# Moving softmax, mask, split and load work in a two-layer hybrid trunk kernel on one core

## The reference: a trunk of two layers

```
for l in range(DEPTH):                       # DEPTH = 2
    x = x + 0.5 * swiglu(rms_norm(x), ...)   # ffn 0, ffn 2
    h = rms_norm(x)
    x = x + (mixer_mla_gdn(h, ...) if l % 2 == 0 else mixer_spatial_gating(h, ...))
    x = x + 0.5 * swiglu(rms_norm(x), ...)   # ffn 1, ffn 3
```

## Time and profile before

| | |
|---|---|
| runs before | median 1094.08 us (1093.31, 1094.08, 1097.67) |
| profiled execution | 1093.22 us, span 1091.2 us, so 2.0 us around it |
| busy in the span | PE 1065.9 us (98%), DVE 637.0 (58%), ACT 514.2 (47%), POOL 49.8 (5%) |
| granted TensorE clock | 0.998 on the mean |
| first mixer | about 201 to 374 us of the span |
| spatial gating | about 752 us on |

### The profile page before, as it was taken

How to read it: one execution, slowest core, us unless ns; L and a number is a source line. 1 busy time by engine, 2 the same in 40 slices (tenths; PEclk the granted TensorE clock), 3 DMA queues, 4 the chain that set the end, 5 groups by cost and what they waited for, 6 DMA issues and landing times.

```text
span 1091.2 us, 18956 instructions
## 1 busy us (share of the span) xinstructions
PE 1065.9 (98%) x8393; PEld 969.9 (89%) x8393; DVE 637.0 (58%) x783; ACT 514.2 (47%) x619; POOL 49.8 (5%) x32
## 2 busy tenths in 40 slices
PE   7999999999888999999999999999999999999998
PEld 7999988998777799998889999887788889999986
DVE  5756543699753675555457655435665547555542
ACT  6644433585673454443345444334665436444430
POOL 1000000110172000000000000001000000000000
PEclk9999999999999999999999999999999999999999
DMA  9856555253005276655538555554554465655531
GB/s 311 268 184 191 193 191 175 92 196 117 2 4 157 78 232 193 193 183 177 184 113 254 178 188 192 194 182 149 192 173 172 165 221 187 187 176 187 191 115 39
DMA packets 127194, 184.88 MB, mean 169 GB/s; under 512 B 4205, under 2 KB 101722, under 8 KB 126986
## 3 DMA queue, kind: packets, MB, share of 16 engines
q1 hardware_dynamic: 126368, 181.85, 51.3%
q0 software_dynamic: 448, 1.71, 0.5%
q10 hardware_dynamic: 298, 0.12, 0.1%
HBM read 182.62 MB, written 1.05 MB: 168 GB/s over the span
## 4 chain that ended last, share of the span: by engine, by line
PE 92%; DVE 4%; issue 2%; ACT 1%; DMA 0%; POOLq 0%; ACTq 0%; POOL 0%; DVEq 0%
PE banks L1337 21%; PE banks L1338 20%; PE banks L1339 20%; PE banks L1378 7%; PE banks L1382 7%; PE banks L1379 7%; PE banks L1735 1%; PE banks L1461 1%; PE banks L1462 1%; PE banks L1463 1%; PE banks L1425 1%; PE banks L1958 1%; DVE wlo L889 1%; DVE arena L1209 1%; DMA pos_rows<-in_positions 0%
## 5 line engine op out<-in xcount | busy, mean ns | idle before, releaser
L889 DVE TENSOR_TENSOR wlo<-raw,whi 128x2048 fp32r<-128x2048 f32 (+1 forms) x167 | 383.4, 2302 | 228.1 <-ACT whi L466 228.0
L466 ACT ACTIVATE whi<-raw 128x2048 fp32r<-128x2048 f32 (+1 forms) x171 | 324.1, 1908 | 382.0 <-PE banks L1339 241.8
L1337 PE MATMUL banks<-xTh,whi 128*128 128x256 f32 x1408 | 397.4, 282 | 1.0 <-DVE wlo L1011 0.9
L1338 PE MATMUL banks<-xTl,whi 128*128 128x256 f32 x1408 | 396.5, 282 | 0.0
L1339 PE MATMUL banks<-xTh,wlo 128*128 128x256 f32 x1408 | 396.5, 282 | 0.0
L1337 PEld LDWEIGHTS banks<-xTh,whi 128*128 128x128 f32 x1408 | 266.2, 189 | 1.7 <-issue 1.3
L1338 PEld LDWEIGHTS banks<-xTl,whi 128*128 128x128 f32 x1408 | 266.3, 189 | 0.0
L1339 PEld LDWEIGHTS banks<-xTh,wlo 128*128 128x128 f32 x1408 | 266.3, 189 | 0.0
L1378 PE MATMUL banks<-whi,hTh 128*128 128x512 f32 x336 | 133.4, 397 | 0.0
L1379 PE MATMUL banks<-wlo,hTh 128*128 128x512 f32 x336 | 132.3, 394 | 0.0
L1382 PE MATMUL banks<-whi,hTl 128*128 128x512 f32 x336 | 105.5, 395 | 0.0
(11 more groups left out here) (249 smaller groups left out, 988.9 us busy)
## 6 DMA issues: line engine op xcount, KB each, us to landing
raw<-in_ffn_w_up SPq DMA_DIRECT2D x44, 1024.0 KB, 5.6
raw<-in_ffn_w_down SPq DMA_DIRECT2D x44, 1024.0 KB, 4.9
raw<-in_ffn_w_gate SPq DMA_DIRECT2D x43, 1024.0 KB, 5.4
raw<-in_sg_w_in SPq DMA_DIRECT2D x16, 1024.0 KB, 5.5
raw<-in_ab_w_in SPq DMA_DIRECT2D x8, 1024.0 KB, 5.2
raw<-in_sg_w_out SPq DMA_DIRECT2D x8, 1024.0 KB, 5.2
raw<-in_ab_w_out SPq DMA_DIRECT2D x4, 1024.0 KB, 4.8
raw<-in_ab_w_in SPq DMA_DIRECT2D x2, 832.0 KB, 4.4
```

Source lines behind the costliest of these rows:

```text
L466: A(whi[:, j % SLOTS, 0:kt * width], raw[:, j % SLOTS, 0:kt * width], ACT.Copy).then_inc(S("hi_ready"), 1)
L889: TT(wlo[:, j % SLOTS, 0:n], raw[:, j % SLOTS, 0:n], whi[:, j % SLOTS, 0:n].bitcast(f32), ALU.subtract).then_inc(S("lo_ready"), 1)
L1337: mm(out_ap, lh, rh, start=first, stop=False)
L1338: mm(out_ap, lh, rl, start=False, stop=False)
```

## The change

1. ACT runs a one-column exponent right after its last SiLU of the convolutions, so that the exponent's table is loaded there, and the last copy `nt_out(5)` moves behind the first head's exponents.
2. DVE takes the sums of gates ahead of `head_sums(1)`, and takes each head's maxima one step earlier than before.
3. The masked blocks of L are made straight from PSUM banks 5 and 2; ACT's copies of L are gone. Two blocks stand at h = 4, the other eight after the last head. The seed of DT for the second tile uses banks 3 and 6, and PE's second `gram` moves behind the last head's values.
4. SP releases the loads of ffn 1 at `o_sums` 2, the middle of the scan.
5. POOL splits b+16 and b+17 in place of DVE. ACT makes the high part of b+16 ahead of the copies of the last transposes (`yT_hi(4, 8)`). PE's eight groups have the feature block outside, so that it is done with b+12 after four groups instead of six.
6. `ws_raw` moves to other memory and is loaded and masked after the first mixer (`x_updated` 8) instead of before the second one. Its memory overlaps `v_norm_row`, which is now loaded after `wsT_ready` 2.

```diff
-        ws_raw = at(0, GROUPS, P)
+        ws_raw = at(R0 + 2912, GROUPS, P)
...
-        DT_SEED_BANKS = ((3, 6), (5, 2))
-        POOL_LO = [u_ab + 12, u_ab + 13, u_ab + 14, u_ab + 15]
+        DT_SEED_BANKS = ((3, 6), (3, 6))
+        POOL_LO = [u_ab + i for i in range(12, 18)]
...
-                sp_.wait_ge(S("w_sums"), 1)
+                sp_.wait_ge(S("o_sums"), 2)
...
             pool_lo(u_ab + 15)
+            pool_lo(u_ab + 16)
+            pool_lo(u_ab + 17)
...
-            pool.wait_ge(S("x_updated"), 16)
-            load(v_norm_row, bc(sg_norm, [P, SGW]), "sg_loaded")
+            pool.wait_ge(S("x_updated"), 8)
             load(ws_raw, sg_ws[0].rearrange("g i j -> i g j"), "sg_loaded")
-            pool.wait_ge(S("sg_loaded"), 32)
+            pool.wait_ge(S("sg_loaded"), 16)
             nc.gpsimd.tensor_tensor(ws_raw, ws_raw, bc(const("tril128").unsqueeze(1), [P, GROUPS, P]),
                                     ALU.mult).then_inc(S("ws_masked"), 1)
+            pool.wait_ge(S("x_updated"), 16)
+            pool.wait_ge(S("wsT_ready"), 2)
+            load(v_norm_row, bc(sg_norm, [P, SGW]), "sg_loaded")
...
             conv_silu(5)
-            nt_out(5)
+            A(rope_tmp[:, 0, 0, 0:1], ones128[:, 0:1], ACT.Exp).then_inc(S("gate_exps"), 1)
...
             exps(0)
+            nt_out(5)
             exps(1)
...
-                if h == 5:
-                    act.wait_ge(S("score_sums"), HEADS)
-                    for t in range(NT):
-                        act.wait_ge(S("seed_sums"), t + 1)
-                        A(LT[:, 512 * t:512 * t + 512], B[(5, 2)[t]][:], ACT.Copy).then_inc(S("seed_ready"), 1)
...
+            hi(b + 16)
             yT_hi(4, 8)
-            for j in range(16, 18):
-                hi(b + j)
+            hi(b + 17)
...
             row_max(1)
-            head_sums(1)
...
-            row_max(2)
             gcf, ekf = (a.rearrange("p t h -> p (t h)") for a in (gc, ek))
...
+            head_sums(1)
+            row_max(2)
...
+            head_norm(QKVn[1], 1, 1.0).then_inc(S("k_normed"), 1)
+            row_max(3)
...
+            def masked_block(t, n):
+                dve.wait_ge(S("seed_sums"), t + 1)
+                if n == 4:
+                    dve.wait_ge(S("score_sums"), HEADS)
+                TT(LT_LEVEL[n][t].rearrange("p (m j) -> p m j", j=64),
+                   B[(5, 2)[t]][:].rearrange("p (m j) -> p m j", j=64), eight(f"level{LEVELS[n]}"), ALU.mult
+                   ).then_inc(S("lt_level"), 1)
...
-                if 0 < h < HEADS - 2:
+                if 1 < h < HEADS - 2:
                     row_max(h + 2)
...
+                    masked_block(0, 0)
+                    masked_block(0, 1)
+
+            for n in range(2, 5):
+                masked_block(0, n)
             for n in range(5):
-                for t in range(NT):
-                    TT(LT_LEVEL[n][t].rearrange("p (m j) -> p m j", j=64), h3(LT, t), eight(f"level{LEVELS[n]}"), ALU.mult
-                       ).then_inc(S("lt_level"), 1)
+                masked_block(1, n)
...
             yT_lo(4, 8)
-            for j in range(16, 18):
-                lo(b + j)
             next_x(2, [1.0, 1.0])
...
-                if h == 7:
-                    pe.wait_ge(S("seed_ready"), 4)
-                    gram(qT, (6, 7))
             weighted_values(HEADS - 1)
+            pe.wait_ge(S("seed_ready"), 4)
+            gram(qT, (6, 7))
...
-            pe.wait_ge(S("seed_ready"), 6)
+            pe.wait_ge(S("lt_level"), 5)
             m1(0, 0)
+            pe.wait_ge(S("lt_level"), 10)
             m1(0, 1)
...
-            for t in range(NT):
-                for kk in range(4):
+            for kk in range(4):
+                for t in range(NT):
```

More of the change, by code:

```diff
@@ L1145, in _ @@
             row_max(1)
-            head_sums(1)
-            dve.wait_ge(S("head_sums"), 2)
-            both = qk_head_ss.rearrange("p a m -> p (a m)")
-            link(rsqrt(both, both, 2 * M, 1.0))
-            def head_norm(a, i, scale):
-                a3 = a.rearrange("p t (h d) -> p (t h) d", d=DK)
-                return STT(a3, a3, scale, bc(qk_head_ss[:, i, :].unsqueeze(2), [P, M, DK]), ALU.mult, ALU.mult)
-            head_norm(QKVn[1], 1, 1.0).then_inc(S("k_normed"), 1)
-            row_max(2)
             gcf, ekf = (a.rearrange("p t h -> p (t h)") for a in (gc, ek))
@@ L1165, in _, with head_norm @@
             ins.then_inc(S("gc_ready"), 1)
+            head_sums(1)
+            row_max(2)
+            dve.wait_ge(S("head_sums"), 2)
+            both = qk_head_ss.rearrange("p a m -> p (a m)")
+            link(rsqrt(both, both, 2 * M, 1.0))
+            def head_norm(a, i, scale):
+                a3 = a.rearrange("p t (h d) -> p (t h) d", d=DK)
+                return STT(a3, a3, scale, bc(qk_head_ss[:, i, :].unsqueeze(2), [P, M, DK]), ALU.mult, ALU.mult)
+            head_norm(QKVn[1], 1, 1.0).then_inc(S("k_normed"), 1)
+            row_max(3)
             m3 = lambda a: a.rearrange("p (m j) -> p m j", j=64)
@@ L1204, in _ @@
                         TT(h3(D, t), eight("eye64"), h3(D, t), ALU.subtract).then_inc(S("d_ready"), 1)
-            dve.wait_ge(S("seed_ready"), 2)
+                    masked_block(0, 0)
+                    masked_block(0, 1)
+            for n in range(2, 5):
+                masked_block(0, n)
             for n in range(5):
-                for t in range(NT):
-                    TT(LT_LEVEL[n][t].rearrange("p (m j) -> p m j", j=64), h3(LT, t), eight(f"level{LEVELS[n]}"), ALU.mult
-                       ).then_inc(S("lt_level"), 1)
+                masked_block(1, n)
             dve.wait_ge(S("exp_done"), 2 * HEADS)
@@ L1745, in m1 @@
             def m1(n, t):
-                pe.wait_ge(S("lt_level"), 2 * n + t + 1)
+                pe.wait_ge(S("lt_level"), 5 * t + n + 1)
                 quadrants(t, (M1_BANKS if n else M1_FIRST)[t], LT_LEVEL[n], natural, by_t(D), d_at(n), flips(9), flips(n)
```

## The result

| | before | changed |
|---|---|---|
| first comparison | 1093.97 us median (1092.70 to 1100.66, 10 runs) | 1102.32 us (1099.14 to 1104.68, 10 runs) |
| ratio, 95% interval | | 1.0055 [1.0036, 1.0073], +6.0 us [3.9, 8.0] |
| profiled execution | 1093.22 us, clock 0.998 | 1102.91 us, span 1101.1 us, clock 0.994 |

Slower, clear of noise, and in all three comparisons by more than 0.5% on the estimate (the intervals reach down to 0.36%). The prediction was 1095.6 us with a range up to 1099.4, so it missed on the slow side. The changed kernel was timed twice more, each time beside the kernel before: 1.0070 [1.0051, 1.0089] and 1.0065 [1.0044, 1.0087]. The three ratios make it +6.0 to +7.7 us.

The account below looks back on a forecast made before the run. PE, busy 98% of the span, was taken as the bound, with about 8 us of waits to win. Terms -1.4 - 2.8 - 1.8 + 4.35 + 1.7 + 2.3 = +2.35 gave 1095.6 us, range 1089.4 to 1099.4.

Parts of the forecast that it names:

- Table and maxima 0: First head's exponents: early table and maxima gain 0, as DVE is full and PE only waits later.
- Masks -1.4: Ten masks before the scan, made from PSUM: they end 1.4 us earlier, shortening PE's 1.6 us wait by that.
- Loads at mid-scan -2.8: Scan: loads released later remove PE's unnamed 1.44 us wait and the low clock, saving 2.8 us.
- Splits -1.8: End of first mixer: DVE's two splits go to POOL, so PE's 1.8 us wait for the update of X goes.
- +4.35: DVE's products at L1286: the second waits on SBUF for POOL's split of b+16, costing PE 4.35 us.
- POOL comes too late: Rival at L1286: POOL's split misses the second product, so the 4.35 us cost goes, giving 1091.2 us; chance 0.27.
- Mask in ffn 1 +1.7: Start of ffn 1: POOL's moved mask holds DVE's row norm, costing 1.7 us; load taken as 3.7 us.
- Gains' load +2.3: Spatial gating, unit b+4: later gains' load delays PE 2.3 us, with the 0.95 us mask wait no longer needed already used up.
- the clock: Rival: TensorE's clock falls in three new idle stretches, some 1.7 us each; 1097.3 to 1100.7 us; chance 0.11.
- a sign of being wrong: Changed kernel's trace: half clock behind the new waits was among the signs that would show the prediction wrong.
- the three prices: Costs at the output gate's products (4.35 us), the mask in ffn 1 (1.7) and the gains' load in gating (2.3).

Follow-up runs that it names:

- f: Kernel before with only the early exponent, later `nt_out(5)` and new order of sums and maxima: 1096.26 us, ratio 1.0003 to before.
- h: Changed kernel with POOL's split and mask held later, gains loaded early, and the old order of table and maxima restored: 1086.53 us, ratio 0.9934 to before.
- a: Changed kernel with POOL's split of b+16 held until DVE's two products are done: 1094.02 us, ratio 0.9995 to before.
- g: Kernel before with only the masked blocks made from PSUM, with their banks and waits: 1092.57 us, ratio 0.9995 to before.
- e: Kernel before with only the loads of ffn 1 released at `o_sums` 2 instead of `w_sums` 1: 1091.48 us, ratio 0.9974 to before.
- m: Changed kernel with unread transposes filling all three new PE waits (products, norm's spread in ffn 1, first gates): 1097.09 us, ratio 1.0030 to before.
- j: Changed kernel with 32 unread transposes on PE ahead of its wait for the output gate's second product: 1099.66 us, ratio 1.0050 to before.
- p: Changed kernel with 23 unread transposes on PE ahead of the first gates of spatial gating alone: 1099.62 us, ratio 1.0052 to before.
- d: Changed kernel with POOL's split held until after the products, gains loaded early, and POOL's mask held later: 1087.50 us, ratio 0.9927 to before.
- i: Kernel before with PE's second `gram` computed twice: 1094.67 us, ratio 1.0007 to before.
- l: Changed kernel unaltered, timed again beside the run with busy work under the products: 1101.79 us, ratio 1.0070 to before.
- n: Changed kernel unaltered, timed a third time beside the runs with busy work at the gates: 1101.25 us, ratio 1.0065 to before.

## Why the prediction was wrong

Its steps, in its own order:

- *Table and maxima 0*: right (f, h, 12.89 against 13.02 us).
- *Masks -1.4*: right for the masks' end where the clock stayed up: 31.41 against 33.02 us in `a`, which is 1.6. The changed kernel's own trace shows 0.5 of it, after a clock fall at 289.7 us, and in time the masks alone (g) gave 0.7 at equal clock.
- *Loads at mid-scan -2.8*: right, -2.73 in the trace and -2.8 by e (of it 1.6 at equal clock, the rest the half clock that goes).
- *Splits -1.8*: the wait for the update of X is gone; *+4.35*: 4.31 longer, 4.4 us of PE's wait. The rival "POOL comes too late" (0.27) is out.
- *Mask in ffn 1 +1.7*: 1.9 us of wait, though the load took 5.3 us and not 3.7: the mask met another instruction of the norm at nearly the same price, which was luck. *Gains' load +2.3*, net of 0.95 (so 3.25 of wait): 2.9 us. The number was close and part of the working was not: ACT's L826 ended 1.1 us later relative to PE, the load was issued 0.6 us after it instead of 0.1, and it landed in 5.1 us. But PE waited only for V's norm, and went through the gates' products while DVE split b+4, where I had put the split on the path too.

So the events were foreseen and the sum of the waits too (9.2 us against 9.3). **The step that failed is the clock.** The sum had no term for it. I kept it as a rival with a chance of 0.11 that stood beside the sum, although the sum itself opened three idle stretches on PE. What I held against it, the 3.1 us at full clock before the first head, was one trace, and the exception: in the four others with that wait the clock fell. It belonged in the sum, behind the 4.4 and the 2.9 us; behind the 1.9 us it fell once in seven traces. The changed kernel's trace has 10.2 us at half clock behind two of the three new waits and 3.4 behind the moved one of 3.0 us, where the sum had none; the prediction had named that as a sign of being wrong. What it is worth follows in two ways. Filling PE's waits took 4.2 us off the changed kernel with the waits' causes left in (m), 2.1 of it at the products (j) and 1.6 at the gates (p, not clear of noise). And by the count, the sum took 3.4 us at half clock out of the kernel before and put none in, while the changed kernel had some 4 us more of it than the kernel before on the mean of the comparisons (15.0 against 10.7): 7.7 us by 0.35, or 2.7 of the 4.5 us by which the prediction fell short of the three comparisons (+6.9 on their mean against +2.4).

A second error is in that rival: one profiled execution of the kernel before, at 0.998, was read as its usual state. Its executions have 10.7 us at 0.50 on the mean (4 to 24 in single ones), and that one 4.4. So a kernel that avoids idle stretches gains more than its trace shows, and d did: -8.0 us against the -6.95 that my terms give with the three prices left out. The rival also lists the new stretches as 4.35, 1.8 and 2.6 us, where my terms make the last one 2.3 + 0.95 = 3.25.

**What stays open.** At equal clock the changed kernel is 5.1 us slower than the kernel before, in both comparisons whose clocks are on record for the two. My sum without the 1.2 us that its removed half clock is worth gives 3.6. So 1.5 us are not the clock. Against the kernel before beside them, and at equal clock, undoing the products' meeting gave 4.2 us, the gains' load 3.9 and the mask 2.3, each with a standard error of about 0.5: 10.4 us where the sum had 9.3, the excess at the gates and the mask. The masks gave 0.7 where it had 1.4. Together that is about the rest, but none of it is large against its error, and the 0.35 is a mean over stretches in which PE sets the pace and others, so a stretch right behind a wait may cost more than that. Nor is it known what decides whether the clock falls in a given execution.

## What to carry to other kernels

When PE is 98% busy, price a new wait of PE at its length plus the chance of a clock fall behind it, read from several traces: here six in six behind 4.4 us, most of the time behind 3 us, once in seven behind 1.9. Here 9.2 us of wait cost 14 to 15 us, 10.4 of them at equal clock, and transposes that nothing reads, put into the waits, gave 4.2 us back; in the wait ahead of the keys' transposes they gave nothing. A split moved to POOL is free only if no DVE instruction on PE's path, with both inputs in SBUF, falls due in its 4.5 us: let POOL wait for that instruction, as `a` does. And compare kernels by several executions with their granted clocks; one execution can differ from the kernel's mean by 2 to 5 us for the clock alone.

## What the runs showed that I had not expected

- The place of the clock's falls differs between executions of one code. Three profiles of the changed kernel have half clock from 289.7 for 3.4, 361.4 for 6.8 and 784.7 for 3.4 us; from 289.2 for 10.2 and 360.9 for 6.8; and from 288.3 for 10.2, 363.4 for 3.4 and 783.2 for 6.8. The 3.1 us of PE's idle time in the earlier trace rows was followed by none in the kernel before, but by 6.8 us of it, from 277.9, in `e` and `i`, and by 3.4 us in `g`, which have the same code there.
- With the masks at half clock the last one came 4 us later in `l` and `n` (35.3 us after the first maximum) than in `a` and `m` (31.4): 10.2 us at 0.50 in a stretch that DVE and PE share went with 0.38 us for each.
- "Issue" waits of PE in the inverse are 0.7 to 3.2 us in all, for nearly the same instructions. The one in the scan, 1.1 to 1.4 us, comes with the weight traffic every time in these traces and never without it.
